# First norms of an encoder layer: scale and bias moved to the eviction of the transposes, residual rows to GpSimd, first convolution chunk split by sequence

## The reference

```python
h = layer_norm(x, ln_in_g, ln_in_b)            # 768 rows of 1024
m = layer_norm(mem, ln_mem_g, ln_mem_b)        # 512 rows of 1024
z = h @ w_in                                   # q 512, k 128, v 128, a 512, gate 512
q, k = rope(rms_norm(q)), rope(rms_norm(k))
att = gqa(q, k, v)                             # 8 heads, 2 kv heads, width 64
u = a * sigmoid(gate)
u = depthwise_conv(u, conv_w) + conv_b         # 31 taps, centred, per sequence
u = silu(layer_norm(u, conv_ln_g, conv_ln_b))
h = layer_norm(2 ** 0.25 * h + concat(att, u) @ w_mix_out, ln1_g, ln1_b)
xa = cross_attention(h, m, w_cq, w_ck, w_cv, w_co)
h = layer_norm(2 ** 0.25 * h + xa, ln2_g, ln2_b)
ff = top-1 group, top-2 experts of 8 in it: (silu(h @ w_gate) * (h @ w_up)) @ w_down
y = layer_norm(2 ** 0.25 * h + ff, ln3_g, ln3_b)
```

## Time and profile before

| | us |
|---|---|
| median of three runs | 1073.58 |
| the profiled execution, device time | 1069.95 |
| its span in the trace | 1068.2 |
| TensorE busy | 947.2 (89% of the span) |
| VectorE busy | 447.0 |
| GpSimd busy | 295.0 |
| ScalarE busy | 228.2 |

### The profile page before, as it was taken

One profiled execution on the slowest core, in us unless ns is written; L12 is line 12 of the kernel. 1 busy time (PEld: TensorE's weight loads), 2 busy tenths in 40 slices (PEclk: granted clock), 3 DMA queues, 4 the chain that ended last, 5 costly groups with the idle time before them and its releaser, 6 DMA issues.

```text
span 1068.2 us, 10055 instructions
## 1 busy us (share of the span) xinstructions
PE 947.2 (89%) x3400; PEld 495.9 (46%) x3400; DVE 447.0 (42%) x716; ACT 228.2 (21%) x547; POOL 295.0 (28%) x344
## 2 busy tenths in 40 slices
PE   4899999699998999999999999957998999999900
PEld 3466465244544444445568545546344444444300
DVE  5599999864623132106234222253321111111156
ACT  2421133234483111101004211130011111111111
POOL 5721033234444222100005321202152111211137
PEclk9999999899999999999999999965998999999965
DMA  9410302203012002211031240152799999999562
GB/s 329 166 40 0 119 1 85 73 1 79 1 38 81 1 0 79 79 39 40 0 140 58 107 188 40 40 238 108 318 402 342 413 421 420 386 411 383 195 240 118
DMA packets 46231, 166.13 MB, mean 156 GB/s; under 512 B 8514, under 2 KB 13890, under 8 KB 33892
## 3 DMA queue, kind: packets, MB, share of 16 engines
q1 hardware_dynamic: 39460, 152.88, 37.2%
q0 software_dynamic: 6720, 12.60, 3.2%
HBM read 157.92 MB, written 18.03 MB: 165 GB/s over the span
## 4 chain that ended last, share of the span: by engine, by line
PE 58%; DVE 3%; POOL 3%; issue 2%; DMA 1%; POOLq 0%; ACT 0%; SPq 0%; DVEq 0%
PE ps L1664 17%; PE ps L2052 8%; PE ps L2081 7%; PE ps L1920 7%; PE ps L2055 5%; PE ps L1842 2%; PE ps L2029 2%; PE ps L1767 2%; PE ps L1742 2%; PE ps L1984 2%; POOL hres L674 1%; PE ps L1673 1%; PE ps L1949 1%; POOL lnc L664 1%; POOL slot_table L882 1%
## 5 line engine op out<-in xcount | busy, mean ns | idle before, releaser
L1664 PE MATMUL ps<-ring,hT 128*128 128x512 f32 (+1 forms) x384 | 145.6, 540 | 0.9 <-issue 0.9
L1208 DVE SCALAR_TENSOR_TENSOR cat<-early,cpar,cat 128x798 f32<-128x798 f32 x120 | 131.2, 1094 | 3.8
L1664 PEld LDWEIGHTS ps<-ring,hT 128*128 128x128 f32 x384 | 72.6, 190 | 71.1 <-issue 68.7
L776 POOL TENSOR_SCALAR hT<-hT,rinv 128x512 f32<-128x512 f32 (+1 forms) x48 | 67.7, 1423 | 96.5 <-DVE rinv L1305 96.5
L1664 PE MATMUL ps<-hT,ring 128*128 128x256 f32 (+1 forms) x256 | 86.0, 499 | 0.8 <-issue 0.7
L842 POOL DMA_INDIRECT pair_rows<-hT,sidx x22 | 22.0, 1001 | 179.1 <-DVE hT L1591 174.1
L1664 PEld LDWEIGHTS ps<-hT,ring 128*128 128x128 f32 x256 | 50.2, 198 | 34.9 <-issue 29.8
L1581 DVE COPY memx<-ps 128x256 f32<-128x256 f32 x22 | 9.3, 424 | 127.0 <-PE ps L2064 124.6
L783 POOL TENSOR_SCALAR memx<-memx,rinv 128x256 f32<-128x256 f32 x24 | 22.1, 924 | 141.8 <-DVE rinv L1263 141.8
L2081 PE MATMUL ps<-ring,memx 128*64 128x512 f32 (+1 forms) x144 | 60.0, 611 | 0.7 <-DVE memx L1581 0.7
L663 POOL TENSOR_SCALAR lnt<-mv 128x1 f32<-128x1 f32 x28 | 10.9, 390 | 174.3 <-DVE mv L691 173.6
(11 more groups left out here) (276 smaller groups left out, 1599.6 us busy)
## 6 DMA issues: line engine op xcount, KB each, us to landing
ring<-w_down SPq DMA_DIRECT2D x16, 1024.0 KB
early<-w_gate SPq DMA_DIRECT2D x12, 1024.0 KB
early<-w_up SPq DMA_DIRECT2D x12, 1024.0 KB
ring<-w_gate SPq DMA_DIRECT2D x10, 1024.0 KB
ring<-w_up SPq DMA_DIRECT2D x10, 1024.0 KB
scr<-w_down SPq DMA_DIRECT2D x8, 1024.0 KB, 15.1
cat<-w_down SPq DMA_DIRECT2D x8, 1024.0 KB
scr<-w_gate SPq DMA_DIRECT2D x5, 1024.0 KB
```

The costliest lines, as they stand in the source:

```text
L776: g.tensor_scalar(sprob[u % 4][:, 0:width], sprob[u % 4][:, 0:width], rinv[:, u % 4:u % 4 + 1], None, ALU.mult).then_inc(prob_ready, 1)
L1208: ins = v.scalar_tensor_tensor(out=acc[:, c, :], in0=src, scalar=cpar[:, c, k:k + 1], in1=acc[:, c, :], op0=ALU.mult, op1=ALU.add)
L1664: last = t.matmul(out_of(bank), lhs(k), rhs(k), start=(k == 0), stop=(k == KC - 1))
```

## The change

Four edits belong together.

1. For x and for the memory rows the gain and bias of the norm are no longer applied to rows. The transposed tile has the channels on the partitions, so the gain and bias are one number per partition: each 128-column piece of a bank is evicted with scale and bias from a small table `lncol`. For x, ScalarE takes the first bank of a tile (four activations of 128 columns) and VectorE the second (four tensor_scalar). For the memory rows ScalarE takes both banks (eight activations). The transposes of x use four PSUM banks in turn in place of two.
2. The residual needs the rows with gain and bias, so GpSimd makes them afterwards: `residual_rows`, two instructions over 1024 columns per x tile, for tiles 0 to 3 ahead of the coefficients of memory tiles 0 and 1, for tiles 4 and 5 behind them. The old `pool_gain` for x tiles 2 to 5 and the four memory tiles goes.
3. Chunk 0's convolution is done for sequence 0 (31 taps of 256 columns) and then for sequence 1 (31 taps of 512), so that it can start when `gates(0, 0)` is done. The statistics of memory tiles 2 and 3 stand behind tap 16 of chunk 1.
4. The convolution's weights arrive already turned; gains and biases for the residual are loaded after the x tiles and not before them; transposes of memory tiles 0, 1 stand after `gates(1, 1)`, and those of tiles 2, 3 after `gates(3, 0)`.

```diff
-            take("tr", ("hT", 0, i, j))
-    take("tr", "cpar")
+            take("first", ("hT", 0, i, j))     # banks 4, 5, 6, 7
...
             sp.dma_start(hres[:, 0, :], x[0:P, :]).then_inc(x_in[0], 16)
-            load_gb(0)
-            for i in range(1, NT):
+            sp.dma_start(hres[:, 1, :], x[P:2 * P, :]).then_inc(x_in[1], 16)
+            sp.dma_start(lncol[:, :, :], ln_cols).then_inc(lncol_in, 16)
+            for n in range(2):
+                sp.dma_start(chunks(ring[:, n, :])[:, :, 0:P],
+                             chunks(w_slabs[n][1], True)[:, :, 0:P]).then_inc(first_in, 16)
+            for i in range(2, NT):
                 sp.dma_start(hres[:, i, :], x[i * P:(i + 1) * P, :]).then_inc(x_in[i], 16)
...
+            for j in range(2):
+                sp.dma_start(xgb[:, j, :], bcast(lnp[j])).then_inc(xgb_in, 16)
+            sp.dma_start(cpar[:, :, :], cpar_dram).then_inc(conv_in, 16)
...
+            def residual_rows(tiles):
+                pool.wait_ge(xgb_in, 32)
+                for i in tiles:
+                    full(pool, ("hT", 0, i, 0))
+                    full(pool, ("hT", 0, i, 1))
+                    link(g.tensor_tensor(hres[:, i, :], hres[:, i, :], xgb[:, 0, :], ALU.mult))
+                    g.tensor_tensor(hres[:, i, :], hres[:, i, :], xgb[:, 1, :], ALU.add).then_inc(resid_done, 1)
+
             norms(LN_X)
+            residual_rows(range(0, 4))
             norms(LN_M[0:2])
+            residual_rows(range(4, NT))
...
+            def first_T(i):                    # on ScalarE, bank 0 of a tile
+                key = ("hT", 0, i, 0)
+                bank = full(act, key)
+                act.wait_ge(lncol_in, 16)
+                for k in range(4):
+                    last = a.activation(hTv[:, k, i * P:(i + 1) * P], bank[:, k * P:(k + 1) * P], ACT.Identity,
+                                        bias=lncol[:, 1, k:k + 1], scale=lncol[:, 0, k:k + 1])
+                last.then_inc(free(key), 1)
...
             gate(0, 0)
             for i in range(2, NT):
-                rows_T(0, i)
+                first_T(i)
+            gate(0, 1)
             act_hat(act, LN_M[0])
             act_hat(act, LN_M[1])
-            gate(0, 1)
             gate(1, 0)
+            gate(1, 1)
             for i in range(2):
                 mem_T(i)
-            gate(1, 1)
+            gate(2, 0)
+            gate(2, 1)
             act_hat(act, LN_M[2])
             act_hat(act, LN_M[3])
-            gate(2, 0)
-            gate(2, 1)
+            gate(3, 0)
             for i in range(2, MT):
                 mem_T(i)
-            for s in range(2):
-                gate(CC - 1, s)
+            gate(3, 1)
...
             mem_rows(LN_M[0:2])
-            for n in LN_M[0:2]:
-                dve_bias(dve, n, link)
-            was_read(dve, "cpar")
-            glu(0)
-            conv(0, 0, 16)
+            dve.wait_ge(conv_in, 16)
+            glu(0, 0)
+            first_conv(0, 0, TAPS)
+            glu(0, 1)
+            first_conv(1, 0, 12)
+            glu(1, 0)
+            first_conv(1, 12, TAPS)
+            glu(1, 1)
+            conv(1, 0, 16)
             mem_rows(LN_M[2:MT])
-            conv(0, 16, 22)
-            glu(1)
-            conv(0, 22, 25)
-            for n in LN_M[2:MT]:
-                dve_bias(dve, n, link)
-            conv(0, 25, TAPS)
-            conv(1, 0, 16)
-            glu(2)
-            conv(1, 16, TAPS)
-            conv(2, 0, 6)
-            glu(3)
-            conv(2, 6, TAPS)
+            conv(1, 16, 28)
+            for s in range(2):
+                glu(2, s)
+            conv(1, 28, TAPS)
+            conv(2, 0, 22)
+            for s in range(2):
+                glu(3, s)
+            conv(2, 22, TAPS)
```

More of the change, by code:

```diff
@@ L152, in take @@
     def take(kind, key):
-        banks = {"mm": (0, 1, 2, 3), "tr": (4, 5), "pv": (6, 7)}[kind]
+        banks = {"mm": (0, 1, 2, 3), "tr": (4, 5), "pv": (6, 7), "first": (4, 5, 6, 7)}[kind]
         b = banks[turn.get(kind, 0) % len(banks)]
@@ L935, in mem_T @@
                     bank = full(act, key)
-                    a.activation(mT[j][:, :, i * P:(i + 1) * P], bank.rearrange("p (k t) -> p k t", k=4),
-                                 ACT.Copy).then_inc(free(key), 1)
+                    for k in range(4):
+                        c = 4 * j + k
+                        last = a.activation(mT[j][:, k, i * P:(i + 1) * P], bank[:, k * P:(k + 1) * P], ACT.Identity,
+                                            bias=lncol[:, 3, c:c + 1], scale=lncol[:, 2, c:c + 1])
+                    last.then_inc(free(key), 1)
             def gate(c, s):
@@ L984, in _ @@
             act.wait_ge(tabs_ready, 1)
+            act.wait_ge(resid_done, NT)
             for what, i in QKV_ORDER:
@@ L1170, in link, with x_stats, first_T @@
                 dve.wait_ge(dve_step, steps[0])
-            for n in LN_X:
+            def x_stats(n):
                 dve.wait_ge(x_in[n], 16)
                 dve_stats(dve, n, link)
-                if n in SHORT:
-                    dve_bias(dve, n, link)
-                elif n - 2 not in SHORT:
-                    dve_bias(dve, n - 2, link)
-            for n in LN_X[-2:]:
-                dve_bias(dve, n, link)
+            def first_T(i):
+                key = ("hT", 0, i, 1)
+                bank = full(dve, key)
+                dve.wait_ge(lncol_in, 16)
+                for k in range(4):
+                    last = v.tensor_scalar(hTv[:, 4 + k, i * P:(i + 1) * P], bank[:, k * P:(k + 1) * P],
+                                           lncol[:, 0, 4 + k:5 + k], lncol[:, 1, 4 + k:5 + k], ALU.mult, ALU.add)
+                last.then_inc(free(key), 1)
+            for n in LN_X[0:3]:
+                x_stats(n)
+            first_T(0)
+            x_stats(LN_X[3])
+            first_T(1)
+            for n in LN_X[4:]:
+                x_stats(n)
+            for i in range(2, NT):
+                first_T(i)
             def mem_rows(ns):
@@ new lines, in tap @@
+            def tap(c, k, at, width, n):
+                src, out = upad[:, c, at + k:at + k + width], acc[:, c, at:at + width]
+                if k == 0:
+                    ins = v.tensor_scalar(out, src, cpar[:, c, 0:1], cpar[:, c, TAPS:TAPS + 1], ALU.mult, ALU.add)
+                else:
+                    dve.wait_ge(conv_done, n)
+                    ins = v.scalar_tensor_tensor(out=out, in0=src, scalar=cpar[:, c, k:k + 1], in1=out,
+                                                 op0=ALU.mult, op1=ALU.add)
+                ins.then_inc(conv_done, 1)
@@ L1210, in conv @@
-                    ins.then_inc(conv_done, 1)
+                    tap(c, k, 0, AW, (c + 1) * TAPS + k)
             def rotate(i):
```

119 lines of the change are left out of this document (56 added, 63 removed).

## The result

The changed kernel takes 1079.12 us (median of six runs, 1077.45 to 1081.21) against 1074.53 (1072.91 to 1076.02) of the kernel before on the same chip: ratio 1.0042, 95% interval 1.0027 to 1.0057. It is slower by 4.6 us. Its profiled execution took 1078.85 us, with a span of 1077.1 and a mean granted clock of 0.939.

A forecast was written before the change was run, and what follows sets the result against it. TensorE bounds nearly everywhere: -8.3 us at the front, a 21.5 wait less 1.5 of transposes, 2.8 for the clock, -9.8 for the filled gap; 4.5 added to the 1073.58 median gives 1078, range 1062 to 1084.

The forecast's parts named there:

- The front: TensorE's start: first transposes at 10.1, `gates(0, 0)` at 16.8, `gates(0, 1)` at 31.7 in place of 39.97, gaining 8.3 us.
- That the front doesn't matter as long as VectorE's start holds: No gain at TensorE's front would not matter, since VectorE's 78 taps set the end.
- The split: Chunk 0's convolution: starts 20.5 us earlier, but 31 taps each of 256 and 512 columns take 39.9 us, not 33.6.
- The collisions: GpSimd row instructions beside VectorE's taps: six of twelve, each costing VectorE 1.97 us, 11.8 us in all.
- C: VectorE's total collision cost before memory tile 2's statistics: 11.8 rows, 2.1 tables, 0.4 tail, together 14.3 us.
- Rival (a): Collisions cost little because 256-column taps leave the port sooner; step 3 13 us earlier, 1060.5 us; chance 0.14.
- The statistics and the wait: Memory tile 2's statistics end at 109.1; TensorE waits from 96.7, `gates(3, 1)` starts at 118.2, lower clock costs 2.8 us.
- What is given back: Gap before self-attention is filled, 9.8 us: products end at 196.7, VectorE is ready at 192, scores come at 200.5.
- step 3: Self-attention scores used as the dating event: 213.6 against 210.01, 3.6 us later, with about 1 us more behind.
- (b): VectorE starts convolution 3 us sooner, or taps and collisions cost 7 us, not 14: -3 us, 1070.5; chance 0.22.
- (c): No change: total collision cost near 10 us, where the sum crosses zero, 1073.6 us; chance 0.12.
- (d): Slower: table instructions cost near 1 us each (+6), TensorE stays longer at lower clock (+2), 1086 us; chance 0.10.

The follow-up runs named there:

- E6: Changed kernel with each transposed bank of x and memory rows evicted in one plain instruction, those norms' gains and biases left out; 1129.1 us, with another expert stage.
- E7: Changed kernel with residual rows of x tiles 3, 4 and 5 moved behind GpSimd's coefficients of memory tiles 2 and 3; 1070.36 us, ratio 0.9963.
- E4: Changed kernel with the split of chunk 0's convolution undone (31 taps of 798 columns), statistics still behind tap 16 of chunk 1; 1075.67 us, ratio 1.0018.
- E2: Changed kernel with GpSimd's residual rows of x tiles 3, 4 and 5 (six instructions) left out; 1066.59 us, ratio 0.9934.
- E9: Changed kernel with chunk 0 whole, statistics of memory tiles 2 and 3 ahead of chunk 1, and four PSUM banks for memory transposes; 1064.99 us, ratio 0.9927.
- E1: Changed kernel with VectorE's statistics of memory tiles 2 and 3 straight after chunk 0, ahead of chunk 1; 1068.26 us, ratio 0.9947.

## Why the prediction was right

The forecast was +4.5 us (1078) and the measurement is +4.6 (1079.12). The mechanism stood as written; several sizes in it were off and cancelled. That the two differ by only 0.1 us is luck: single terms were off by up to 1.8 us, and the table above ties the traced event to the medians only within 1.6.

- **The front.** First transposes at 10.27 (10.1 forecast), `gates(0, 0)` at 17.25 (16.8), `gates(0, 1)` at 32.20 (31.7): 7.8 us gained, 8.3 forecast. The mis-sized term is the eviction in four pieces: 1.51 us on ScalarE and 1.33 on VectorE where I took 0.8 from a row of 287 ns for a single piece. That row is of a plain one; a piece on ScalarE here takes 472 to 498 ns by its own record, as a mean of each group. ScalarE's pieces of the first tile and of memory tile 2, in the kernel after:

```profile
11.40 1.51 ACT L958 ACTIVATE hT<-ps,lncol 128x128 f32<-128x128 f32 x4
115.02 1.51 ACT L970 ACTIVATE gb<-ps,lncol 128x128 f32<-128x128 f32 x4
```

- **That the front doesn't matter as long as VectorE's start holds.** Shown by E6 for TensorE's part: of its lead of 7.2 us at the end of `gates(3, 0)` all but VectorE's 2.5 went into the wait. But VectorE's start does hang on the front: with short evictions it came 4.4 us earlier.
- **The split.** In E7, where no row instruction is beside them, the 62 taps take 16.8 and 24.0 us; less the 0.8 for the tables this is 40.0, as forecast (39.9), so its +6.3 for the fixed parts stands. The head start was counted rightly as well, but not weighed against doing the chunk whole: E4 shows that this has the statistics 3 us earlier.
- **The collisions.** Six row instructions beside taps, the other six done by 35.5: as forecast. Their price is 2.0 us each (E2, E7) and 1.97 was forecast from the two taps of the earlier trace rows. The 2.1 us for the table instructions and the tail of 0.4 were too much: 0.8 was measured. C is 12.8, not 14.3. Rival (a), that a short tap and a row instruction pass each other, is refuted: six cost the same beside taps of 256 and of 798. The Trainium skill's rule ("SBUF — State Buffer", section "Who interferes with whom") is full exclusion for the instruction's length; the runs agree in kind, and its 2.35 each stays 0.35 above what they show.
- **The statistics and the wait.** At 107.16 and ended at 108.7 (109.1 forecast: 1.5 less for the collisions, 0.7 more for a later start, 0.4 at the glus). TensorE's wait began at 98.5 (96.7), since two memory tiles took 4.15 and not 3 us, again the evictions; transposes of tile 2 at 111.35 (111.6), `gates(3, 1)` at 118.88 (118.2). The granted clock behind the wait was 0.51 until 122.8, and cost 15.85 - 13.90 = 2.0 us there (E9 has the same products in 13.90); 2.8 was forecast.
- **What is given back.** The products ended at 196.49 (196.7), VectorE was ready at 191 (192), the first scores came at 199.70 (200.5), step 3 at 213.08 (213.6), and the wait for VectorE that was to add 1 us behind it added 0.6: step 4 is 3.65 late.
- **The other rivals.** (b) gave -3 us for a VectorE that is 3 us sooner or pays 7 us less. E4 has it 3 us sooner and stands at +1.9, so the first half of (b) was wrong: that case is only less slow. E2 has 12 us less and stands at -7.2. Between them a microsecond of VectorE is worth about one of time, so the sum would cross zero some 4.6 us below the measured 12.8, at C near 8 (an estimate), and not near 10 as (b) and (c) have it. In (d) the table instructions were to cost 1 us each; they cost 0.1, and the lower clock cost 2.0 and not 4.8.

What the forecast didn't ask is how cheaply the loss could be had back. E1 shows that the order alone decides the sign: three statistics instructions per tile behind 62 taps in place of 78.

## What to carry to other kernels

When one engine runs ahead, look for the small instruction that it will next need from an engine full of long work, and put it ahead of that work: here it was worth 10 us (E1). A head start for a busy engine is worth nothing if it has to be bought with more instructions and moves that engine's work beside an instruction that stalls it; an idle stretch can be the cheaper place for the other's work (E4). A gain at the front is worth only what the next wait does not swallow, so date a change by one event behind all its waits and follow that.

## What the runs showed of the hardware

- A GpSimd instruction over 1024 columns with two inputs in SBUF costs VectorE 2.0 us beside taps of 256 columns and beside taps of 798 alike; GpSimd itself takes 2.35 to 2.5 us beside the short ones and 3.0 to 3.1 beside the long ones.
- Not every VectorE instruction pays. Beside such a row instruction (33.18 to 35.5) the statistics of a memory tile ran at their usual length, while the first tap, a TENSOR_SCALAR over 256 columns with one input in SBUF, took 2.32 us (0.41 alone, in E7). Statistics beside a row instruction, of the kernel after, VectorE then GpSimd:

```profile
33.41 1.24 DVE L698 BATCH_NORM_STATS2 stats<-memx 128x6 f32<-128x512 f32 x2
33.18 2.35 POOL L762 TENSOR_TENSOR hres<-hres,scr 128x1024 f32<-128x1024 f32 x1
```

- GpSimd instructions over 128 columns (0.6 us each) beside taps of 256 cost VectorE 0.1 us each: a tap is lengthened from 485 to 565 ns, at most to 694. Beside taps of 798 columns (E4) it is GpSimd that pays: such an instruction takes it 1.1 us, and VectorE loses 0.6 us over all ten.
- Scale and bias per partition at a PSUM eviction come at four instructions per bank: 1.51 us on ScalarE against 0.6 for the bank in one. The Trainium skill ("VectorE: DVE Perf Modes", section on the TRN2 errata) prices a ScalarE instruction that reads PSUM at 172 cycles and one per column at 1.2 GHz, which is an estimate of 1.0 us for four pieces of 128; the trace has half as much again.
